# A two-block transformer kernel on one core: a tenth weight slot for the experts, constants multiplied at four norms, a last pair worked by halves

## The reference

```python
y = (silu(x @ w_gate[e]) * (x @ w_up[e])) @ w_down[e]   # 1024x512, 1024x512, 512x1024
x = x + gate2 * sum over the two experts of weight * y
return rms_norm(x, g_final)
```

## Time and profile before

| what | value |
|---|---|
| median of 3 runs | 1464.62 us (1463.04 to 1466.13) |
| the profiled execution | 1464.04 us |
| its span, first to last instruction | 1462.0 us |
| PE busy | 1363.4 us, 93% of the span |
| DVE, ACT busy | 703.9 us (48%), 560.7 us (38%) |
| mean granted clock of PE | 0.962 of full speed |
| moved by DMA | 372.57 MB |

### The profile page before, as it was taken

How to read it: one execution, slowest core, us unless ns; L and a number is a source line. 1 busy time by engine, 2 the same in 40 slices (tenths; PEclk the granted TensorE clock), 3 DMA queues, 4 the chain that set the end, 5 groups by cost and what they waited for, 6 DMA issues and landing times.

```text
span 1462.0 us, 20083 instructions
## 1 busy us (share of the span) xinstructions
PE 1363.4 (93%) x7942; PEld 996.6 (68%) x7942; DVE 703.9 (48%) x1234; ACT 560.7 (38%) x859; POOL 43.8 (3%) x59
## 2 busy tenths in 40 slices
PE   5999898999999998899997997878999999999996
PEld 5988587888777997899985985564444445444442
DVE  4754545666656444677755655533322322322222
ACT  4344535555554575665645534321111111111112
POOL 1000000111000000000000002000000000000000
PEclk9999999999999999999998998589999999999998
DMA  8556343899853631355644451293999999999994
GB/s 305 179 208 246 123 136 126 306 305 324 319 173 115 231 116 58 124 173 174 243 170 146 139 207 59 72 392 127 428 427 428 429 430 426 429 429 429 427 428 187
DMA packets 110232, 372.57 MB, mean 255 GB/s; under 512 B 4300, under 2 KB 59884, under 8 KB 97504
## 3 DMA queue, kind: packets, MB, share of 16 engines
q1 hardware_dynamic: 102272, 344.07, 60.8%
q0 software_dynamic: 7904, 27.76, 5.5%
HBM read 370.75 MB, written 1.05 MB: 254 GB/s over the span
## 4 chain that ended last, share of the span: by engine, by line
PE 78%; DMA 10%; DVE 8%; ACT 3%; issue 1%; SPq 0%; ACTq 0%; DVEq 0%
PE ps L538 15%; PE ps L1261 11%; PE ps L502 8%; PE ps L503 8%; PE ps L504 8%; PE ps L1283 6%; DMA arena<-in_w_expert_up_dram 4%; DMA ring<-in_w_expert_gate_dram 4%; PE ps L517 3%; PE ps L519 3%; PE ps L518 3%; PE ps L1244 3%; DVE w_low L439 2%; PE ps L938 2%; PE ps L1296 1%
## 5 line engine op out<-in xcount | busy, mean ns | idle before, releaser
L439 DVE TENSOR_TENSOR w_low<-ring,w_high 128x1024 fp32r<-128x1024 f32 x260 | 306.8, 1221 | 237.7 <-ACT w_high L431 228.2
L431 ACT ACTIVATE w_high<-ring 128x1024 fp32r<-128x1024 f32 x264 | 264.8, 1051 | 235.4 <-PE ps L538 101.9
L502 PE MATMUL ps<-h_high,w_high 128*128 128x256 f32 x1088 | 312.8, 288 | 6.8 <-DVE w_low L439 6.2
L503 PE MATMUL ps<-h_low,w_high 128*128 128x256 f32 x1088 | 308.7, 284 | 0.0
L504 PE MATMUL ps<-h_high,w_low 128*128 128x256 f32 x1088 | 308.4, 283 | 0.0
L502 PEld LDWEIGHTS ps<-h_high,w_high 128*128 128x128 f32 x1088 | 209.6, 193 | 26.3 <-issue 18.4
L503 PEld LDWEIGHTS ps<-h_low,w_high 128*128 128x128 f32 x1088 | 209.8, 193 | 0.0
L504 PEld LDWEIGHTS ps<-h_high,w_low 128*128 128x128 f32 x1088 | 209.5, 193 | 0.0
L1261 PE MATMUL ps<-ring,arena 128*64 128x512 f32 x656 | 183.7, 594 | 6.6 <-DMA arena<-in_w_expert_gate_dram 2.4
L1261 PEld LDWEIGHTS ps<-ring,arena 128*64 128x64 f32 x656 | 58.8, 137 | 99.2 <-issue 94.2
L1261 PE MATMUL ps<-arena 128*64 128x512 f32 x368 | 120.1, 594 | 2.5 <-DMA ring<-in_w_expert_gate_dram 1.4
(11 more groups left out here) (332 smaller groups left out, 1520.1 us busy)
## 6 DMA issues: line engine op xcount, KB each, us to landing
ring<-in_ffn_w_up_dram SPq DMA_DIRECT2D x44, 1024.0 KB, 7.8
ring<-in_w_expert_gate_dram SPq DMA_DIRECT2D x21, 2048.0 KB, 23.6
ring<-in_w_expert_down_dram SPq DMA_DIRECT2D x20, 2048.0 KB, 25.1
ring<-in_w_expert_up_dram SPq DMA_DIRECT2D x20, 2048.0 KB, 24.3
arena<-in_w_expert_up_dram SPq DMA_DIRECT2D x12, 2048.0 KB, 24.3
ring<-in_ret_w_in_dram SPq DMA_DIRECT2D x11, 2048.0 KB, 8.1
arena<-in_w_expert_gate_dram SPq DMA_DIRECT2D x11, 2048.0 KB, 23.5
ring<-in_ffn_w_down_dram SPq DMA_DIRECT2D x10, 2048.0 KB, 9.0
```

Source lines behind the costliest of these rows:

```text
L431: nc.scalar.activation(hi, raw, ACT.Copy).then_inc(hi_done, 1)
L439: last = eng.tensor_tensor(lo, raw, hi.bitcast(F32), ALU.subtract)
L502: nc.tensor.matmul(o, hi, hTh[:, k, :], start=(k == 0), stop=False)
L503: nc.tensor.matmul(o, hi, hTl[:, k, :], start=False, stop=False)
```

## The change

1. **Tenth slot.** `x` and `hT` become two views of one 2 MB buffer `x_hT`, which is appended to the homes as number 9: `NS` is 10. SP loads tile 9 into it once `t_lg` is 2. The final output goes to `xn`, and the squares' unused product to a piece of the arena.
2. **Turns of five pairs.** All loops of the expert stage write out TURN = 5 pairs and turn three times; SP's write out 30 loads and turn twice, and the other 24 loads before the last two tiles are straight code.
3. **Constants multiplied.** `idle_turns(n)` issues n matmuls of 128x128 by 128x512 constants into PSUM bank 3 ahead of the wait in `norm_pe`: 5 at norm 1, 5 at norm 3, 10 at norm 5, 7 at norm 6.
4. **Queries on VectorE.** DVE scales the queries out of PSUM, ahead of its next `split_low`; ACT's copy goes.
5. **The last pair by halves.** PE finishes the first 512 columns of the down product before the second and signals each (`m_half`, `m_dn`). DVE and ACT treat one half and then the other, and PE scatters by half, with `m_fin` after the last two matmuls. The dummy `Sqrt` for the final norm moves from before the last pair to right before the final loop.

```diff
+        x_hT = sb("x_hT", [P, NT * D + KD * T])
+        x = x_hT[:, 0:NT * D].rearrange("p (t d) -> p t d", t=NT)
+        hT = x_hT[:, NT * D:].rearrange("p (k t) -> p k t", k=KD)
...
+        def idle_turns(n):
+            for _ in range(n):
+                nc.tensor.matmul(ps[:, 3, :], ident, const[:, 0:C], start=True, stop=True)
+
-        def norm_pe(pe, r):
+        def norm_pe(pe, r, turns=0):
             n = N_TR[r]
+            idle_turns(turns)
             pe.wait_ge(norm_xn, NT * (n + 1))
...
-        ring += [carve(ARENA - (3 - n) * SLOT, SLOT) for n in range(3)]
+        ring += [carve(ARENA - (3 - n) * SLOT, SLOT) for n in range(3)] + [x_hT[:, :]]
...
-        HOMES = (2, 6, 7, 8, 0, 1, 3, 4, 5)
-        NS = len(HOMES)
+        HOMES = (2, 6, 7, 8, 0, 1, 3, 4, 5, 9)
+        NS, TURN = len(HOMES), 5
...
+                elif home == 9:
+                    sp.wait_ge(t_lg, 2)
...
-                trips = (TILES - 2 - first) // 18
+                trips = (TILES - 2 - first) // (6 * TURN)
...
-            norm_pe(pe, 1)
+            norm_pe(pe, 1, 5)
-            norm_pe(pe, 3)
+            norm_pe(pe, 3, 5)
-            norm_pe(pe, 5)
+            norm_pe(pe, 5, 10)
-            norm_pe(pe, 6)
+            norm_pe(pe, 6, 7)
...
-                down(homes, (0, 1))
+                for half in range(2):
+                    down(homes, (0, 1), half)
                 for e in range(2):
                     enter_tile(6 * j + 4 + e)
-                down(homes, (2, 3)).then_inc(m_dn, 1)
-                scatter(j)
+                down(homes, (2, 3), 0).then_inc(m_half, 1)
+                down(homes, (2, 3), 1).then_inc(m_dn, 1)
+                last_scatter(j)
...
+            def last_scatter(j):
+                pe.wait_ge(m_swt, j + 1)
+                for half in range(2):
+                    for y, done in ((y_hi, m_ya), (y_lo, m_yv)):
+                        pe.wait_ge(done, 2 * j + 1 + half)
+                        for t in range(NT):
+                            last = add_rows(t, y, half)
+                            if half and y is y_lo:
+                                last.then_inc(m_fin, 1)
...
                 split_high(act, *(("sb_qk", 2 * u + 2) if u < 3 else ("sb_out", 0)))
-                nc.scalar.activation(sqk[:, u, :], ps[:, 0, :], ACT.Copy, scale=SDH ** -0.5).then_inc(sqk_fa, 1)
...
-            nc.scalar.activation(credit[:, 7:8], const[:, 0:1], ACT.Sqrt)
             expert_end(0)
             with act.If(most > R):
...
+            nc.scalar.activation(credit[:, 7:8], const[:, 0:1], ACT.Sqrt)
             for t in range(NT):
                 act.wait_ge(m_fin, t + 1)
...
+                wide_done(dve, halves["sb_qk"] + 2 * u + 1)
+                nc.vector.tensor_scalar(sqk[:, u, :], ps[:, 0, :], SDH ** -0.5, None, ALU.mult).then_inc(s_q_kept, 1)
                 split_low(dve, *(("sb_qk", 2 * u + 2) if u < 3 else ("sb_out", 0)))
...
+            def last_gated(j):
+                for half in range(2):
+                    dve.wait_ge(*((m_dn, j + 1) if half else (m_half, j // PAIRS + 1)))
+                    gate(half)
+                    dve.wait_ge(m_ya, 2 * j + 1 + half)
+                    low(half)
```

More of the change, by code:

```diff
@@ L248, in build @@
         iota = k_("iota")
-        ring_in = [sem(f"ring_in{s}") for s in range(9)]
+        ring_in = [sem(f"ring_in{s}") for s in range(10)]
         half_in = [sem(f"half_in{e}") for e in range(2)]
@@ L390, in arrivals @@
             return 16 * sum(len(units[m][2]) for m in range(n + 1) if units[m][1] == slot)
-        last_fill = [arrivals(holder[s]) if s < 3 else 0 for s in range(9)]
+        last_fill = [arrivals(holder[s]) if s < 3 else 0 for s in range(10)]
         def token_major(phase, h):
@@ L608, in build @@
         GROUPS = SH // 2
[L609 to L610 removed]
+        s_q_kept, s_k_kept, sv_a, sv_v, s_hide = (
+            sem("s_" + n) for n in ("q_kept", "k_kept", "v_a", "v_v", "hide"))
         s_z, s_l, s_sp, s_in, s_a, s_o, s_ot = (
@@ L674, in build @@
         xg = carve(1408, KD, P)
+        squares = carve(1408, 2, C)
         hs = carve(2432, DE)
@@ L758, in expert_load @@
                 s, value, step = used(N - NS)
-                sp.wait_ge(s, value if i is None else i * (3 * step) + value)
+                sp.wait_ge(s, value if i is None else i * (TURN * step) + value)
                 dst, src, done = expert_tile(N, i)
@@ L1277, in turn_hidden, with down, add_rows, scatter @@
                 last.then_inc(m_ht, 1)
[L1279 to L1285, removed]
-                return last
[L1288 to L1292, removed]
+            def down(homes, ks, half):
+                for k in ks:
+                    for e in range(2):
+                        last = nc.tensor.matmul(ps[e * R:(e + 1) * R, 6 + half, :], hgT[:, k, e * R:(e + 1) * R],
+                                                tall[homes[e]][:, k, half * C:(half + 1) * C],
+                                                start=(k == 0), stop=(k == KE - 1), skip_group_check=True)
+                return last
+            def add_rows(t, y, half):
+                return nc.tensor.matmul(ps[:, 2 * t + half, :], selT[:, t * P:(t + 1) * P], y[:, half * C:(half + 1) * C],
+                                        start=False, stop=False, skip_group_check=True)
+            def scatter(j, i):
+                pe.wait_ge(m_swt, at(j + 1, i, TURN))
+                pe.wait_ge(m_ya, at(2 * j + 2, i, 2 * TURN))
+                pe.wait_ge(m_yv, at(2 * j + 2, i, 2 * TURN))
                 for t in range(NT):
@@ L1295, in scatter @@
                         for half in range(2):
[L1296 to L1301, removed]
+                            last = add_rows(t, y, half)
+                last.then_inc(m_sct, 1)
+            def last_scatter(j):
[4 more added lines that the diff above has]
+                        for t in range(NT):
+                            last = add_rows(t, y, half)
+                            if half and y is y_lo:
+                                last.then_inc(m_fin, 1)
             def expert_pass(r):
@@ L1308, in expert_pass @@
                 turn_select(first)
-                with pe.Fori(0, PAIRS // 3) as i:
-                    for j in range(first, first + 3):
+                with pe.Fori(0, PAIRS // TURN) as i:
+                    for j in range(first, first + TURN):
                         gate_or_up(j, 1, i)
@@ L1634, in expert_pass @@
                 silu(first)
-                with act.Fori(0, PAIRS // 3) as i:
-                    for j in range(first, first + 3):
+                with act.Fori(0, PAIRS // TURN) as i:
+                    for j in range(first, first + TURN):
                         xg_evict(j + 1, i)
@@ L2195, in expert_pass @@
                 turned(first)
-                with dve.Fori(0, PAIRS // 3) as i:
-                    for j in range(first, first + 3):
+                with dve.Fori(0, PAIRS // TURN) as i:
+                    for j in range(first, first + TURN):
                         hidden(j, i)
```

99 lines of the change are left out of this document (51 added, 48 removed).

## The result

The changed kernel takes 1450.13 us (median of 10 runs, 1447.5 to 1458.41), the kernel before, run beside it, 1463.63 us (median of 10, 1460.01 to 1466.77). The ratio is 0.9918, 95% interval 0.9896 to 0.994: 12.0 us faster, between 9 and 15. Two of the ten runs took 1458.3 and 1458.4 us at a mean granted clock of 0.965, the other eight at most 1452.65 at 0.969 to 0.976; neither of the two was profiled, and why they took longer stays open.

What follows compares the result with a forecast made beforehand. DMA's expert-weight stream sets the end, with PE only 8.5 us behind. Gains of 4.9 + 0 + 0 + 2.0 + 2.7 = 9.6 us put the median at 1455.0 us, range 1448.0 to 1460.5.

Steps and rivals of the forecast that it cites:

- the slot: Expert weight stream: a tile loaded early, while DMA idles, brings every later tile 4.9 us sooner; bounds 0 and 4.9.
- the constants: Norms 1, 3, 5 and 6: filler matmuls delay nothing and partly keep PE's clock; 2.0 us gained, bounds 0 and 9.3.
- the last pair: Pair 15 to the end: earlier squares and no table load before the root; 2.7 us gained, bounds 1.3 and 3.2.
- moves the wait and not the end: Rival, expert stage: PE becomes the bound, up to 4.9 us missing, 1457.5 to 1459.9 us; chance 0.14.
- The turns of five: Expert loops: fewer jumps back, which show no price, so the longer turns were costed at nothing.
- the rival of PE's code: Expert loop's jumps back: PE must load code each turn; with 10 us at each, 1471.4 us; chance 0.05.
- At full clock a matmul of this very shape takes 3.67 / 8 = 0.44 us: Step sizing the norms' filler: 5, 10 and 7 matmuls take 2.2, 4.4 and 3.1 us.
- the first rival: Clock is kept at all four norms: 9.3 us gained instead of 2.0, so 1447.7 us; chance 0.13.
- a sign of being wrong: Norms 5 and 6: transposes of 1.9 us, with router matmuls in 3.5 us, would show the forecast wrong.
- the prediction's own sum for a kept clock: Gain if all four norms keep PE's clock: 1.1 + 1.1 + 1.8 + 5.3 = 9.3 us.
- the discount: Norms 5 and 6 counted at only 0.3 us each, since the gaps left would mostly still let the clock fall.
- The queries: Scaling queries on DVE instead of ACT: gain 0, at most 0.6 us each way at one of four steps.

## Why the prediction was right, and where it wasn't

The forecast's direction and range held, and so did its account of the slot. Its number came out of errors of both signs: the constants gave much more than their term, the last pair nothing. That they nearly cancel is luck.

**The slot** (forecast 4.9). Measured 4.1 to 4.5: from pair 0's down to pair 15's it takes 413.9 to 414.3 us in the eight profiles with the slot and PE's branch where it was, and 418.4 to 418.6 in the three without it and in the one with its load held back. The stream has 2.10 MB less and is 4.15 us shorter; at the 425.7 GB/s of before a tile is 4.93, and the rate of the shorter stream was 425.0, which takes back 0.8. The tile comes at 982 and not at 994, since what lies ahead of it was 12 us shorter in this profile. PE's up matmuls of pair 15 start 415.95 us behind those of pair 0, where it was 420.07: over 15 steps of 27.43 us that is 4.5 us of waits for weights, where it was 8.6 and the forecast had 3.6. The rival "moves the wait and not the end" is out: the last up tile lands at 1415.05 and its matmuls start at 1415.19, so DMA still sets the end.

**The turns of five** (forecast nothing at the jumps). Right in the loop: in the profile after, q8 carries four blocks of 16 KB from 1000 to 1108 us and one at 1108.4, all in the first turn, and then none to 1410. PE's pairs keep their step, so the rival of PE's code is out at the jumps. The Trainium skill (Advanced Engine Details and Errata, ISA Cache) gives TensorE 128 KB; the rows agree in that the five pairs' loop, five blocks of 16 KB, ran without reloads. Wrong was that the longer loop is free. It puts 1.9 to 2.05 us of wait on ACT, once, behind the branch after the loop: there with turns of five in both orders of the last pair (1.87 and 2.05 in the old, 2.01, 1.92, 1.89 and 1.94 in the new), absent with turns of three in both, absent when the branch comes earlier. In the old order it lay almost wholly beside PE's scatter (tail 16.92 and 17.11 against 16.72), in the new order it is bare (15.70 against 14.19, and 17.53 against 15.89: 1.5 to 1.6 us). That section of the skill gives the engines other than TensorE 32 KB; no run here measures that size. That the idle time is a fetch of code, and not another cost of the same jump, is argued and not shown: packets of 8 KB stand in q14 at 1435.6 and 1436.4, inside it, but two such packets stand at the same place with turns of three (1439.55 and 1440.19), beside a table load that nothing held up.

**The constants** (forecast 2.0). This is the term that was mis-sized, by 6 us, and its step is "At full clock a matmul of this very shape takes 3.67 / 8 = 0.44 us". The row with x8 was four matmuls (two groups by two halves in the source). At 0.88 each the constants fill the gaps almost wholly, the mechanism of the first rival (chance 0.13) is what happened, with transposes of 1.97 us at norms 5 and 6, which the forecast had named as a sign of being wrong. The four norms give 1.12 + 1.09 + 1.13 + 4.91 = 8.25 us in the profile, where the prediction's own sum for a kept clock was 1.1 + 1.1 + 1.8 + 5.3 = 9.3. At norm 5 the 1.8 were right, since the mixer's first matmul comes 1.67 us earlier; the 1.13 has 0.54 us of a slower mixer in it. Counted at the norm, the four give 8.8. The assumption behind the discount, that 3.9 and 4.6 us of gap let the clock fall, held in the one profile that had such gaps (4.40 and 4.70 us, half the constants). One reading of the earlier trace rows is off: a mean clock of 0.68 from 235 to 236 puts the rise at 235.6 and not at 235.4, and nothing hangs on it.

**The last pair** (forecast 2.7 shorter, measured 0.8 longer from the first down matmul on; from the end of the last one, as the forecast counts, 13.93 us became 13.06). This is the step whose result failed: the sum took 7.11 us for the down product and a table load right behind the last rounding. The steps of the order held: the tail with the clock kept and no wait of ACT is 14.19 us against 16.72, so 2.53. Two things took it back. ACT's wait took 1.6. The other is the clock: PE idles 2.56 us between the up and the down product but for four transposes, and of ten profiles with that gap the clock fell in six, the changed kernel's among them, for 3.4 us. That costs 1.7 to 1.8 us in the new order, whose down product is on the path from its first half on, and 0.7 in the old (17.45 with the constants alone against 16.72). With one constant in the gap it was kept in three of three.

| tail, us | clock kept | clock fell |
|---|---|---|
| old order, turns of three | 16.72 | 17.45 |
| old order, turns of five | 16.92, 17.11 | |
| new order, turns of five | 15.70 | 17.53, 17.44, 17.45 |
| new order, no wait of ACT | 14.19, 14.43, 14.19 | 15.89, 15.87 |

So the new order alone is worth 1.2 to 1.4 us with turns of five if the clock stays. If it falls, no profile has the old order with turns of five to set beside the 17.44 to 17.53; with turns of three it was 15.87 against 17.45. The Trainium skill's price for a table switch (ScalarE: Activation LUTs, What ACT_TABLE_LOAD costs), 2.66 us in all, is not seen here: the load takes 1.28 us from 1437.32 and the dummy root follows at 1438.62, and where ACT has no wait the load itself stands 0.02 us behind the rounding (1434.55, ACT's branch early).

**The queries** (forecast 0): 0, to 0.05 us at an equal clock.

**The sum.** -8.25 - 4.14 + 0.82 = -11.6 us by the stretches, and -12.0 by the ratio. The forecast's -9.6 was near because 6 us too little for the constants stood against 3.5 us too much for the tail and 0.8 for the slot.

## What to carry to other kernels

Before a duration is taken from a row, count its records against the instructions in the source: a float32 matmul with 512 columns of constants showed as two. Here filler for an idle PE paid when it closed the gap nearly whole (at most 1.01 us left) and hardly with 2.9 to 4.7 us left, so size it by a measured length, and look at what stands behind the gap at half clock. When a loop gets longer, look at the first branch behind it on every engine: an engine may stand idle there, probably for its code, and that costs when a reordering takes away the work that hid it, or when the clock falls over it, as it did here after 2.33 us.

## What was not expected of the hardware

- Idle time behind a branch, put down to code but not shown to be that, cost ACT 1.9 to 2.05 us and PE 1.89 us beyond its weights, with packets of instructions of 8 KB (0.3 to 0.55 us each) and 16 KB (0.9 to 1.8 us) about it.
- With one 16 KB packet of instructions across the output's first transfer, the two transfers landed in 3.3 to 4.1 us (mean of the two), where they took 2.6 without one.
- Idle gaps of the same 2.56 us ahead of the down product let PE's clock fall to 1.2 GHz in six profiles and kept it at 2.4 in four. Why the one and why the other stays open.
